# A layer's modulation products moved from TensorE to VectorE, with one TensorE sum over the rows for each column group

## What is computed

```python
mod = jax.nn.silu(c) @ ada_w + ada_b          # c: (1, 1024), ada_w: (1024, 6144)
shift1, scale1, gate1, shift2, scale2, gate2 = jnp.split(mod[:, None, :], 6, axis=-1)
h = rmsnorm(x, norm1_w) * (1 + scale1) + shift1
proj = h @ w_in
...                                            # gated delta (4 heads) and sparse attention (4 heads) on proj
x = x + gate1 * (mixed @ w_out)
h2 = rmsnorm(x, norm2_w) * (1 + scale2) + shift2
```

## Time and the profile before

| | |
|---|---|
| median of 3 runs | 3889.66 us (3888.75 to 3892.39) |
| the profiled execution | 3896.1 us, span of the trace 3894.2 us |
| TensorE busy | 3602.6 us (93%) |
| VectorE busy | 2025.6 us (52%) |
| ScalarE busy | 1239.4 us (32%) |
| the start, to the scaling loop | 85.1 us |
| the mixer | 355.6 to 730.5 us |

### The profile page before, as it was taken

One profiled execution on the slowest core, in us unless ns is written; L12 is line 12 of the kernel. 1 busy time (PEld: TensorE's weight loads), 2 busy tenths in 40 slices (PEclk: granted clock), 3 DMA queues, 4 the chain that ended last, 5 costly groups with the idle time before them and its releaser, 6 DMA issues.

```text
span 3894.2 us, 43152 instructions
## 1 busy us (share of the span) xinstructions
PE 3602.6 (93%) x18120; PEld 3021.5 (78%) x18120; DVE 2025.6 (52%) x3470; ACT 1239.4 (32%) x1609; POOL 0.2 (0%) x4
## 2 busy tenths in 40 slices
PE   7788888789998776999999899999999999999998
PEld 6568888568887665998878687888888878888886
DVE  2661443465653344466653428868696634444444
ACT  1233211232222332345552222444444422222222
POOL 0000000000000000000000000000000000000000
PEclk9895788899999888899999999999999999999999
DMA  5121111212223122212223334464645475555552
GB/s 190 54 77 68 53 55 55 76 65 92 94 101 104 41 69 87 99 64 77 76 82 135 141 135 136 138 200 137 200 138 189 153 273 194 190 189 188 191 194 76
DMA packets 211313, 474.63 MB, mean 122 GB/s; under 512 B 10272, under 2 KB 141856, under 8 KB 175024
## 3 DMA queue, kind: packets, MB, share of 16 engines
q1 hardware_dynamic: 208960, 463.89, 34.6%
q10 hardware_dynamic: 2160, 7.99, 0.5%
HBM read 380.61 MB, written 91.23 MB: 121 GB/s over the span
## 4 chain that ended last, share of the span: by engine, by line
PE 76%; DVE 8%; ACT 4%; issue 1%; DMA 1%; SPq 0%; DVEq 0%; ACTq 0%
PE bank L537 69%; PE bank L1004 3%; DVE wl L492 1%; PE bank L593 1%; PE bank L2150 1%; PE bank L549 1%; ACT wh L485 1%; ACT sgm L2218 1%; PE bank L1247 0%; DVE nq L149 0%; PE bank L2159 0%; DVE nr L623 0%; DVE AT L1194 0%; DVE hl L617 0%; ACT sgm L2222 0%
## 5 line engine op out<-in xcount | busy, mean ns | idle before, releaser
L537 PE MATMUL bank<-hh,wh 128*128 128x512 f32 (+1 forms) x2512 | 984.6, 392 | 62.9 <-DVE hl L617 32.9
L492 DVE TENSOR_TENSOR wl<-ring,wh 128x2048 fp32r<-128x2048 f32 (+2 forms) x250 | 556.9, 2228 | 832.0 <-ACT wh L485 832.0
L537 PE MATMUL bank<-hl,wh 128*128 128x512 f32 (+1 forms) x2512 | 953.9, 380 | 0.0
L537 PE MATMUL bank<-hh,wl 128*128 128x512 f32 (+1 forms) x2512 | 951.6, 379 | 0.0
L485 ACT ACTIVATE wh<-ring 128x2048 fp32r<-128x2048 f32 (+2 forms) x250 | 465.4, 1862 | 1109.3 <-PE bank L537 1064.9
L537 PEld LDWEIGHTS bank<-hh,wh 128*128 128x128 f32 x2512 | 482.3, 192 | 175.1 <-issue 56.7
L537 PEld LDWEIGHTS bank<-hl,wh 128*128 128x128 f32 x2512 | 482.4, 192 | 91.5 <-issue 7.7
L537 PEld LDWEIGHTS bank<-hh,wl 128*128 128x128 f32 x2512 | 481.6, 192 | 91.6
L537 PE MATMUL bank<-pl,wh 128*128 128x512 f32 x1024 | 403.5, 394 | 0.0
L537 PE MATMUL bank<-ph,wh 128*128 128x512 f32 x1024 | 401.4, 392 | 0.0
L537 PE MATMUL bank<-ph,wl 128*128 128x512 f32 x1024 | 397.3, 388 | 0.0
(11 more groups left out here) (456 smaller groups left out, 4260.3 us busy)
## 6 DMA issues: line engine op xcount, KB each, us to landing
ring<-in_v SPq DMA_DIRECT2D x68, 1024.0 KB, 4.9
ring<-in_u SPq DMA_DIRECT2D x64, 1024.0 KB, 5.5
gelu_spill<-gst SPq DMA_DIRECT2D x128, 256.0 KB, 2.4
weight_spill<-stage SPq DMA_DIRECT2D x32, 1024.0 KB, 8.9
gv<-gelu_spill SPq DMA_DIRECT2D x64, 512.0 KB, 4.1
wv<-weight_spill SPq DMA_DIRECT2D x64, 512.0 KB, 5.7
ring<-in_ada SPq DMA_DIRECT2D x24, 1024.0 KB, 4.9
ring<-in_wup SPq DMA_DIRECT2D x22, 1024.0 KB, 4.8
```

The costliest lines, as they stand in the source:

```text
L492: v.then_inc(v.e.tensor_tensor(wl[q % 2][:, 0:n], ring[k % 4][:, 0:n], wh[q % 2][:, 0:n].bitcast(F32), S_), s("parts"))
L537: ins = p.e.matmul(out, l, r, start=start and i == 0, stop=stop and i == len(pairs) - 1, skip_group_check=not check)
```

## The change

A modulation tile is now summed over its eight row tiles on VectorE, each multiplied by its column of `scv` as a per-partition scalar: one multiply and seven multiply-adds on 128x256 fp32, each waiting for the one before. TensorE then makes two products of the accumulator (128x128 blocks) by a column of ones. A ring tile is free after VectorE's last sum. At the start there are eight accumulators, in the mixer two. The norm's squares and sums come ahead of the modulation on ScalarE and TensorE, and VectorE takes the mean after tile 4. The three loads of the ScalarE queue have a semaphore each, and cols goes first. In the mixer a tile's operations are spread over three steps of `attn_ve` (3, 3 and 2 of them), and its TensorE part is at the head of `attn_pe`'s group, ahead of the PV product. The meta rows' norm runs ahead of the two streams, instead of behind the tiles. `CHAINS` is packed anew (left out here).

```diff
+    mod_acc = lambda i: acc0[i] if i < 8 else acc1[i % 2]
+
+    def ada_ve(v, i, k0, k1):
+        v.wait_ge(s("scv"), 1)
+        v.wait_ge(s(f"ring{SLOT['ada', i] % 4}"), 16 * (SLOT["ada", i] // 4 + 1))
+        if i >= 10 and k0 == 0:
+            v.wait_ge(s("ada"), i - 1)
+        w, out = ring[SLOT["ada", i] % 4][:, :].rearrange("p (k n) -> p k n", k=8), mod_acc(i)[:, :]
+        for k in range(k0, k1):
+            if k == 0:
+                ins = ts(v.e, out, w[:, 0, :], scv[:, 0:1], M)
+            else:
+                v.settle()
+                ins = stt(v.e, out, w[:, k, :], scv[:, k:k + 1], out, M, A_)
+            v.then_inc(ins, s("ada_sum") if k == 7 else s("ve"))
+        gone("ada", i, s("ada_sum"), i + 1)
+
+    def ada_pe(p, i):
+        p.wait_ge(s("ada_sum"), i + 1)
+        for j in range(2):
+            c = 2 * i + j
+            ins = mm(p, pm[:, c:c + 1], [(mod_acc(i)[:, 128 * j:128 * j + 128], C["ones"][:, 0:1])], check=False)
+        p.then_inc(ins, s("ada"))
 
     def first_pe(p):
-        p.wait_ge(s("consts"), 48)
-        run(ada_pe(p, 0, 8))
+        p.wait_ge(s("consts"), 16)
         norm_pe(p, 0)
+        for i in range(8):
+            ada_pe(p, i)
 
     def first_sc(a):
+        a.e.dma_start(cols[:, :], D["cols"]).then_inc(s("cols").sem, 16)
         a.e.dma_start(cst[:, :], D["consts"]).then_inc(s("consts").sem, 16)
-        a.e.dma_start(cols[:, :], D["cols"]).then_inc(s("consts").sem, 16)
-        a.e.dma_start(mT[:, :, :], D["metaT"]).then_inc(s("consts").sem, 16)
-        a.wait_ge(s("consts"), 48)
+        a.e.dma_start(mT[:, :, :], D["metaT"]).then_inc(s("meta").sem, 16)
+        a.wait_ge(s("cols"), 16)
         a.then_inc(a.e.activation(scv[:, :], cc["c"], ACT.Silu), s("scv"))
         a.wait_ge(s("x0"), 16)
+        a.wait_ge(s("consts"), 16)
+        norm_roots(a, 0, x0, None)
         high(a, 0)
         high(a, 1)
-        norm_sc(a, 0, x0, None)
+        a.wait_ge(s("meta"), 16)
+        norm_high(a, 0)
         end_sc(a)
 
     def first_ve(v):
-        v.wait_ge(s("consts"), 48)
+        v.wait_ge(s("cols"), 16)
+        for i in range(8):
+            ada_ve(v, i, 0, 8)
+            if i == 4:
+                norm_mean(v, 0)
         v.wait_ge(s("ada"), 8)
+        v.wait_ge(s("consts"), 16)
...
     def attn_pe(p):
         for n in range(51):
             if n >= 5 and n % 3 == 2:
                 g = (n - 5) // 3
                 mt = g // 4
-                p.wait_ge(s("at_pt"), 3 * g + 3)
                 if g:
                     p.wait_ge(s("at_lo"), g)
+                else:
+                    p.wait_ge(s("me_h"), 1)
+                ada_pe(p, 8 + g)
+                p.wait_ge(s("at_pt"), 3 * g + 3)
...
             if n >= 5 and n % 3 == 2:
                 lower((n - 5) // 3)
+            if 2 <= n < 50:
+                ada_ve(v, 8 + (n - 2) // 3, *((0, 3), (3, 6), (6, 8))[(n - 2) % 3])
             yield
...
-    RATES = 1, 0.42, 0.14
+    RATES = 1, 0.42
 
     def mixer_pe(p):
         arrive(p, 2)
-        together((gdn_pe(p), RATES[0]), (attn_pe(p), RATES[1]), (then(ada_pe(p, 8, 24, sums), meta_pe(p)), RATES[2]))
+        run(meta_pe(p))
+        together((gdn_pe(p), RATES[0]), (attn_pe(p), RATES[1]))
```

More of the change, by code:

```diff
@@ L308, in _build @@
         nb[0] = norm_bufs(0, ar)
+        acc0 = [sb(f"mod_acc{j}", [128, 256], F32, ar) for j in range(8)]
     with ExitStack() as ar:
@@ L335, in _build @@
             gates = sb("gates", [128, 4, 12], F32, a2)
+            acc1 = [sb(f"mod_acc1_{j}", [128, 256], F32, a2) for j in range(2)]
             nmt = [sb(f"nmt{j}", [128, 16], F32, a2) for j in range(2)]
@@ L594, in norm_pe, with norm_roots @@
                        s("st_mm"))
-    def norm_sc(a, i, src, ready, whole=False):
+    def norm_roots(a, i, src, ready):
         nt, nq, nr = nb[i]
@@ L605, in norm_sc, with norm_high @@
         a.then_inc(a.e.activation(nr[:, :], nr[:, :], ACT.Sqrt), s("st_rs"))
-        if whole:
-            return
+    def norm_high(a, i):
+        nt, nq, nr = nb[i]
         for k in range(8):
@@ L610, in norm_sc, with norm_mean @@
             a.then_inc(a.e.activation(hh[:, k, 16:528], nq[k % 3][:, :], ACT.Copy), s("hi"))
+    def norm_sc(a, i, src, ready, whole=False):
+        norm_roots(a, i, src, ready)
+        if not whole:
+            norm_high(a, i)
+    def norm_mean(v, i):
+        nr = nb[i][2]
+        v.wait_ge(s("st_mm"), 8 * i + 8)
+        v.then_inc(ts(v.e, nr[:, :], bank[6][:, :], 1.0 / 1024, M, EPS, A_), s("ve"))
+        v.settle()
+        v.then_inc(v.e.reciprocal(nr[:, :], nr[:, :]), s("st_rc"))
     def norm_ve(v, i, src, wcol, shift=None, out=None):
@@ L618, in lower @@
                        s("h"))
[L620 to L623, removed]
+        if i:
+            norm_mean(v, i)
         v.wait_ge(s("st_rs"), i + 1)
@@ L683, in first_ve @@
         v.settle()
[L684 to L685 removed]
+        v.then_inc(stt(v.e, scl[:, 0:8], modc[:, 8:16], 1.0, cc["norm1"], A_, M), s("mods"))
+        v.settle()
         low(v, 0)
@@ L1225, in span_of @@
         return 31 if branches[n][2] == 0 else 128 * (branches[n][0] + 1)
-    sums = []
     def attn_pe(p):
@@ L1240, in attn_pe @@
                 p.then_inc(mm(p, pm[:, 128:256], pairs, check=False), s("at_pv"))
-                sums.append(g)
             if n < 48:
@@ L1337, in meta_pe @@
             p.wait_ge(s("me_sq"), k + 1)
-            if sums:
-                p.wait_ge(s("at_lo"), len(sums))
             p.then_inc(p.e.matmul(bank[7][:, 64:80], C["ones"], nmt[k % 2][:, :], start=k == 0, stop=k == 7,
@@ L1366, in meta_ve @@
         v.then_inc(v.e.tensor_tensor(hl[:, :, 0:16], q16[:, :, :], hh[:, :, 0:16].bitcast(F32), S_), s("me_h"))
-    def ada_idle():
-        for _ in range(16):
-            yield
-    def then(a, b):
-        yield from a
-        yield from b
-    RATES = 1, 0.42, 0.14
+    RATES = 1, 0.42
     def mixer_pe(p):
         arrive(p, 2)
-        together((gdn_pe(p), RATES[0]), (attn_pe(p), RATES[1]), (then(ada_pe(p, 8, 24, sums), meta_pe(p)), RATES[2]))
+        run(meta_pe(p))
+        together((gdn_pe(p), RATES[0]), (attn_pe(p), RATES[1]))
     def mixer_sc(a):
@@ L1385, in mixer_sc @@
         a.wait_ge(s("gsp"), 16)
-        together((gdn_sc(a), RATES[0]), (attn_sc(a), RATES[1]), (then(ada_idle(), meta_sc(a)), RATES[2]))
+        run(meta_sc(a))
+        together((gdn_sc(a), RATES[0]), (attn_sc(a), RATES[1]))
         next_high(a, "win1t", 0)
@@ L1393, in mixer_ve @@
         v.wait_ge(s("gsp"), 16)
-        together((gdn_ve(v), RATES[0]), (attn_ve(v), RATES[1]), (then(ada_idle(), meta_ve(v)), RATES[2]))
+        run(meta_ve(v))
+        together((gdn_ve(v), RATES[0]), (attn_ve(v), RATES[1]))
         next_low(v, "win1t", 0)
```

55 lines of the change are left out of this document (28 added, 27 removed), and 7 rows, old and new, of the table CHAINS.

## The result

The changed kernel takes 3786.9 us (3782.85 to 3790.7, four runs) against 3889.2 (3888.67 to 3892.39): a ratio of 0.9735 [0.9722, 0.9748], 102.3 us less. That is faster, inside the predicted range of 3733 to 3818, and 26 us above the forecast of 3761. It is nearly the number of rival 1 (3789), for reasons that are in part others than that rival's. The profiled execution has a span of 3787.7 us.

The account below looks back on a forecast made before the run. TensorE, busy 93%, was taken to bound the kernel overall, and one dependent chain its start. Savings of 29 (start), 93 (mixer groups), 1 (first group) and 6 (tail), 129 us, took 3889.7 to 3761 us; range 3733 to 3818.

Parts of the forecast that it names:

- rival 1: Mixer: VectorE's added work is serial ahead of what TensorE waits for, 16.4 us a group, 3789 us in all; chance 0.20.
- The start: Up to the projection's scaling loop: the new chain begins that loop at 55 us instead of 85; 29 us saved, ends 33 and 22.
- The mixer, removed and added: Attention groups: VectorE becomes limiting by a small margin, 14.5 us a group instead of 20.7; 93 us saved, ends 118 and 65.
- the two ends 12.8 and 16.4: Mixer group, us: VectorE's work with only the waits for `exp` and `hi`, or everything added put on TensorE's chain.
- slack of four steps: Mixer: TensorE is at most 4 lane steps ahead of VectorE, so 14.5 us was taken instead of the lower end.
- Meta rows: Their norm, moved from the mixer's end to its front: costs about 5.5 us there, saves 6 at the end (3 to 9).
- The first group: Mixer's first group: loses 5.5 us to the meta rows, sheds its old 6.8 us modulation tile; net 1 us shorter.
- Rival 2: Mixer: TensorE's clock falls in the gaps, to a mean of 0.75; 18.9 us a group, 3827 us in all; chance 0.13.
- Rival 3: Mixer: the clock stays at 1.2 GHz throughout; 23.9 us a group, 3902 us in all; chance 0.03.
- Rival 4: Mixer: near-ideal overlap of VectorE and TensorE, 12.8 us a group, 3736 us in all; chance 0.06.
- signs of the forecast: Mixer signs included: groups' stretch 218 us instead of 310, VectorE over 80% busy, granted clock above 0.9.
- the limit named for being wrong: Mixer: the forecast is wrong at 17 us a group or more; the clock then tells rival 1 from Rival 2.

Follow-up runs that it names:

- e5: The changed kernel with all eight sums of a mixer tile in one block where VectorE waited, and the product one group later; 3737.3 us.
- e1: The changed kernel with TensorE's product of a modulation tile one attention group later, VectorE's sums left in place; 3759.8 us.
- e9: The changed kernel with eight unused 128x128 products added on TensorE in each group, ahead of the product that waits for the sums; 3771.5 us.
- e2: The changed kernel with seven of the eight VectorE operations of each mixer tile left out, so its modulation is not the full sum; 3729.4 us.
- e6: The changed kernel with the meta rows' norm moved back behind the two streams; 3790.2 us.
- e4: The changed kernel with the norm's mean on VectorE after modulation tile 5 instead of tile 4; 3788.4 us.
- e3: The changed kernel's new start with the old mixer (modulation on TensorE, meta rows behind it); 3854.4 us.
- e10: The changed kernel's new mixer with the old start (tiles 0 to 7 on TensorE); 3814.6 us.
- e7: The changed kernel with the edits of e5 and e4, but tile 8's sums placed in VectorE's wait for the meta rows' sums; 3737.9 us.

## Why the prediction was right or wrong

**The start: right.** 29 us were taken, 30.5 came, and the first projection product stands at 57.8 (58 forecast). The tile's duration (3.96 us against 4.05) and the eight sums (9.72 against 9.8) fit; the hole was 4.05 us and not 3, since tile 4 landed at 24.9 instead of 25.8 and was done sooner, and the mean came at 33.0 as forecast. `scv` came at 6.94, not before 6. VectorE did wait for it and began at 7.25 (8 forecast), but it cost nothing, as tile 1 then waited 1.09 us for its transfer. The straight line between two rows for 256 columns held: 0.485 us for one multiply-add. The Trainium skill's formula for two-tensor operations (VectorE: DVE Perf Modes, the TRN2 errata) gave an estimate of 0.42 us and a tile of 3.6; the measurement decides for the row.

**The mixer: the step "The mixer, removed and added" gave 14.5 us a group and 93 us in all; measured were 16.26 and 66.** The loads were right. TensorE's own work was put at 11.5 us a group, and e5, where the clock is up, has 171.2 / 15 = 11.4. VectorE's was put at 12.0, and the change has 171.6 / 15 = 11.4. What was wrong was the term for how they overlap: 14.5 was a value picked between the two ends 12.8 and 16.4, not a sum, and the only price for the wait for `ada_sum`, 0.5 us, stood in the upper end. That wait is 2.2 us in 13 of 16 groups. What the runs showed in place of the overlap:

- The product stands one attention step behind its last sums, and PV and the next scores stand behind the product. VectorE's next work needs those scores. So each engine works while the other waits; neither is over 81% busy. The "slack of four steps" didn't help, since it is one between lane steps, while this cycle runs through the attention stream.
- e1 removes this wait alone: 14.45 us. That this is the 14.5 of the forecast is luck, as the forecast was for the kernel with the wait in it. e5 has the same work in another place: 13.05, near the lower end of 12.8. Which end came was decided by the place of the sums and of their product, and that could be read from the diff.
- That the measured 16.26 is so near the upper end of 16.4 is luck in part. The end was 11.5 us of TensorE's work plus all of VectorE's added work; measured were 13.2 us busy (197.5 / 15, at a granted clock of 0.86) and 3.1 idle.
- The clock. The gaps expected near 1 us were 2.2, and by e9 the clock's part is about 1.0 of the 1.8 us a group.

The whole from 20.7 downwards, in us a group: 16.26 the change; 15.30 with the clock kept up (e9); 14.45 without the wait (e1); 13.05 with the sums in VectorE's idle time (e5); 12.24 without most of the sums (e2).

**Meta rows: right in both terms,** 6.0 at the front and 7.2 at the end for 5.5 and 6 (e6). The first group was to be 1 us shorter and was 0.9 longer (20.9 against 20.0). The term that failed there is the old modulation tile, put at 6.8 us: in e6, with the meta rows at the end, the first group is 14.9, so the tile's going gave 5.1, net of the new product and sums. The stretch from the last PV product to the mixer's end is 37.1 us, from 44.1, a gain of 7 for 6.

**The sum by the traces:** 30.5 + 66.4 - 0.9 + 7.0 = 103 us up to the mixer's end (627.1 against 730.0), of 129 forecast. Of the missing 26 the groups are 26.6 (93 - 66.4) and the first group 1.9; the start and the tail gave 1.5 and 1.0 more than forecast.

**The rivals.** Rival 1 had the time, and the mechanism in part: the sums stand in front of what TensorE waits for, but without that wait they cost 2.2 us of their 3.6 (e1, e2). Its sum had TensorE at full clock with all of VectorE's work behind it, while part of the measured 16.26 is the clock. Rival 2 took part: behind 12 of the 13 waits the clock is down, though the mean of the groups rose from 0.79 to 0.86. Its sum is wrong, however. At a mean granted clock of 0.75, 11.5 us of work take 11.5 / 0.75 = 15.3 us and not 17.3, with the same waits 16.9 a group, a saving of 57 and a time of 3797; so this rival lay only 10 us from the measured time and inside the stated range. Rival 3 did not occur. Rival 4 is close to e5, not to the change. Of the signs of the forecast, three failed: the stretch of the groups is 243.8 us and not 218, VectorE is at 70% and not over 80%, the clock at 0.86 and not over 0.9. All say that the overlap failed in part, while the limit named for being wrong, 17 us a group, wasn't reached. So the time lies in the range, 26 us above the forecast, with the overlap in the groups not as the forecast had it.

**Left open.** Why the same TensorE instructions take longer in one profiled execution than in another, in e4's groups and behind the mixer.

## What to carry to other kernels

When work is moved to an engine with free time, find in the trace the instruction ahead of which that engine is idle, and put the work just there and a full period ahead of its reader: the same eight operations cost 4.0 us a group spread over the steps and 0.8 in the idle time. A new wait is priced by what stands behind it on both engines, round to the waiting engine's supplier, and not by its own length. Two engines that are each 70 to 80% busy, as here, can be in such a cycle and not near a limit: the same work then took 13.05 us a group instead of 16.26.

## What the runs showed of the hardware that was not expected

More TensorE work made the kernel faster: with eight 128x128 products put into a wait of 2.2 us, the granted clock went from 0.86 to 0.95, the PV products behind it from 390 to 296 ns, and the time from 3786.9 to 3771.5 us. In the group shown, the PV products ran at a granted clock of 0.50 behind an idle time of 2.13 us, and at 1.00 with the wait filled.

And the same instructions, from the mixer's end to the end of the span, took 3147.9 us (e5), 3151.4 and 3151.6 (e3, e10), 3160.6 (the change) and 3164.0 (e1, e7) in single profiled executions, and those between scaling loop and mixer 267.2 to 271.2. An edit that is worth less than some 10 us can't be read in the total. It is to be read in its own stretch of the trace, and there beside TensorE's busy time for the same records, since even that stretch moves by 3 to 4 us with the clock.
